# Layer-1 local attention: low weight pieces moved behind the exponentials and the scaling, pair 6's norm factor ahead of the last square, pair 7's sums and mean ahead of an output tile

## What is computed

```python
def swa_mixer(h, wq, wk, wv, q_norm_w, k_norm_w, sinks, wo):
    q = rms_norm((h @ wq).reshape(b, l, kv, grp, d), q_norm_w) * (d ** -0.5)
    k = rms_norm((h @ wk).reshape(b, l, kv, d), k_norm_w)
    v = (h @ wv).reshape(b, l, kv, d)
    ...
    s_meta = jnp.einsum('bnikgd,bjkd->bnkgij', qb, km)
    s_band = jnp.einsum('bnikgd,bnjkd->bnkgij', qb, kband)
    s_band = jnp.where(valid, s_band, -jnp.inf)
    p = sink_softmax(jnp.concatenate([s_meta, s_band], -1), sink)
    orr = (jnp.einsum('bnkgim,bmkd->bnikgd', p[..., :N_META], vm)
           + jnp.einsum('bnkgij,bnjkd->bnikgd', p[..., N_META:], vband))
    return jnp.concatenate([om, orr], 1) @ wo
```

## Time and profile before

| | |
|---|---|
| median of 3 runs | 1246.34 us (1246.31 to 1250.26) |
| profiled execution | 1246.21 us, of which its span 1244.4 us |
| PE busy | 1219.0 us (98%), 9378 matmuls |
| DVE busy | 897.7 us (72%) |
| ACT busy | 695.2 us (56%) |
| POOL busy | 179.7 us (14%) |
| chain that ended last | PE 89%, DVE 6%, ACT 3% of the span |

### The profile page before, as it was taken

One profiled execution on the slowest core, in us unless ns is written; L12 is line 12 of the kernel. 1 busy time (PEld: TensorE's weight loads), 2 busy tenths in 40 slices (PEclk: granted clock), 3 DMA queues, 4 the chain that ended last, 5 costly groups with the idle time before them and its releaser, 6 DMA issues.

```text
span 1244.4 us, 25767 instructions
## 1 busy us (share of the span) xinstructions
PE 1219.0 (98%) x9378; PEld 1136.2 (91%) x9378; DVE 897.7 (72%) x1670; ACT 695.2 (56%) x1272; POOL 179.7 (14%) x214
## 2 busy tenths in 40 slices
PE   7999999999999989999999999999999999999997
PEld 7999999999999889999989999888889879888887
DVE  7688688788546869888756667977555797877453
ACT  7667355555434656555544555777444586777432
POOL 0343150000112333000011004000011105000100
PEclk9999999999999999999999999999999999999999
DMA  8323357776544336566654444666666523665662
GB/s 293 103 86 110 96 152 236 205 200 198 190 154 120 103 121 207 183 185 196 209 167 146 132 147 145 199 185 186 189 185 183 186 83 120 201 186 170 202 186 69
DMA packets 60449, 205.80 MB, mean 165 GB/s; under 512 B 6096, under 2 KB 14544, under 8 KB 60240
## 3 DMA queue, kind: packets, MB, share of 16 engines
q1 hardware_dynamic: 56048, 200.33, 52.5%
q10 hardware_dynamic: 4320, 4.35, 1.1%
HBM read 200.46 MB, written 4.19 MB: 164 GB/s over the span
## 4 chain that ended last, share of the span: by engine, by line
PE 89%; DVE 6%; ACT 3%; issue 1%; POOL 0%; DMA 0%; ACTq 0%; DVEq 0%
PE bank L331 27%; PE bank L327 21%; PE bank L329 17%; PE bank L330 17%; DVE w_lo L279 1%; DVE cb L700 1%; PE bank L1642 1%; PE bank L1619 1%; PE bank L1632 1%; ACT w_hi L270 1%; ACT sm_s L1699 1%; DVE sm_d L1657 0%; ACT sm_d L1699 0%; PE bank L1294 0%; DMA raw<-w_mix_in 0%
## 5 line engine op out<-in xcount | busy, mean ns | idle before, releaser
L279 DVE TENSOR_TENSOR w_lo<-raw,w_hi 128x1024 fp32r<-128x1024 f32 (+1 forms) x357 | 461.1, 1293 | 167.1 <-ACT w_hi L270 166.5
L331 PE MATMUL bank<-x,w_lo 128*128 128x256 f32 (+2 forms) x1776 | 503.8, 284 | 0.0
L270 ACT ACTIVATE w_hi<-raw 128x1024 fp32r<-128x1024 f32 (+1 forms) x357 | 386.1, 1084 | 207.5 <-PE bank L331 198.5
L329 PE MATMUL bank<-x,w_hi 128*128 128x272 f32 (+2 forms) x1264 | 365.5, 289 | 8.0 <-DVE x L405 8.0
L330 PE MATMUL bank<-x,w_hi 128*128 128x272 f32 (+2 forms) x1264 | 360.4, 285 | 0.0
L331 PEld LDWEIGHTS bank<-x,w_lo 128*128 128x128 f32 x1776 | 334.5, 188 | 0.1
L329 PEld LDWEIGHTS bank<-x,w_hi 128*128 128x128 f32 x1264 | 239.0, 189 | 10.2 <-DVE w_lo L279 8.0
L330 PEld LDWEIGHTS bank<-x,w_hi 128*128 128x128 f32 x1264 | 238.8, 189 | 0.4
L327 PE MATMUL bank<-x,w_hi 128*128 128x512 f32 x512 | 181.4, 397 | 0.0
L327 PE MATMUL bank<-m,w_hi 128*128 128x512 f32 x448 | 157.4, 393 | 0.0
L331 PE MATMUL bank<-m,w_lo 128*128 128x256 f32 x512 | 144.8, 283 | 0.0
(11 more groups left out here) (338 smaller groups left out, 1784.6 us busy)
## 6 DMA issues: line engine op xcount, KB each, us to landing
raw<-w_up SPq DMA_DIRECT2D x88, 512.0 KB, 4.3
raw<-w_mlp_up SPq DMA_DIRECT2D x64, 512.0 KB, 4.2
raw<-w_mlp_down SPq DMA_DIRECT2D x64, 512.0 KB, 4.2
raw<-w_down SPq DMA_DIRECT2D x32, 704.0 KB, 4.1
raw<-w_mix_in SPq DMA_DIRECT2D x29, 512.0 KB, 3.9
raw<-w_moba_in SPq DMA_DIRECT2D x24, 512.0 KB, 4.3
raw<-w_swa_in SPq DMA_DIRECT2D x12, 512.0 KB, 3.6
raw<-w_mix_out SPq DMA_DIRECT2D x8, 512.0 KB, 3.5
```

Of the source, the lines that this page charges most:

```text
L270: nc.scalar.activation(w_hi[:, slot, 0:WIDTHS[g]], raw[:, slot, 0:WIDTHS[g]], ACT.Copy).then_inc(hi_ready, 1)
L279: nc.vector.tensor_tensor(w_lo[:, slot, 0:WIDTHS[g]], raw[:, slot, 0:WIDTHS[g]], w_hi[:, slot, 0:WIDTHS[g]].bitcast(F32), ALU.subtract).th ...
L329: nc.tensor.matmul(out, whi, xh, start=(chunk == 0), stop=False)
L331: mm = nc.tensor.matmul(out, wlo, xh, start=False, stop=end)
```

## The change

Three things move; no instruction is added or removed. First, in steps 1 to 5 ACT makes the `w_hi` piece after the exponentials, and in steps 0 to 5 DVE makes the `w_lo` piece after the scaling `norm`, ahead of the tile's eviction. Second, POOL takes pair 6's power ahead of the square of query tile 7. Third, PE does the head sums of pair 7 ahead of the partial output tile of step 6, and ACT takes their mean ahead of pair 6's exponentials.

```diff
@@ dve_swa @@
                     if p < 6:
+                        norm(p, 0, 2)
                         dve_rest(dve, lin.piece0 + (6 if p else 5) + p + AHEAD)
-                        norm(p, 0, 2)
                     else:
@@ act_swa @@
                 if p < HEADS // 2:
-                    if 0 < p < 6:
+                    if p == 6:
+                        squares_mean(p + 1)
+                    pair_exps(act, swa, p)
+                    if p < 6:
                         act_round(act, lin.piece0 + 6 + p + AHEAD)
-                    pair_exps(act, swa, p)
                     if p in (4, 7):
                         lag_copy(p // 7)
-                    if p == 0:
-                        act_round(act, lin.piece0 + 6 + AHEAD)
-                    if p + 1 < HEADS // 2:
+                    if p < 6:
                         squares_mean(p + 1)
-                    else:
+                    elif p == 7:
                         act.wait_ge(S("rel_stored"), 16 * 8)
@@ pool_swa @@
-                if 1 < t < 7:
+                if t > 1:
                     rsqrt(t - 1)
...
-            rsqrt(6)
             lag_queries(1)
@@ pe_swa @@
                 if p == 6:
+                    query_sums(p + 1)
                     pe.wait_ge(evac_done, SWA0 + 11)
                     pe_tile(pe, out, 0, ready=early, part=(0, 4))
...
-                if p + 1 < HEADS // 2:
+                if p < 6:
                     query_sums(p + 1)
```

## The result

| | before | changed |
|---|---|---|
| median (8 runs each) | 1246.72 us (1246.07 to 1250.26) | 1250.72 us (1248.40 to 1251.66) |
| profiled execution | 1246.21 us, span 1244.4 | 1248.40 us, span 1246.6 |
| ratio | | 1.0022, interval 1.0012 to 1.0032 |

The change makes the kernel about 0.2% slower. The two medians alone have a ratio of 1.0032, the upper end of the interval. I measure local attention from PE's first scores (402.37 in the profile before, 402.19 in this one) to DVE's first residual tile behind it (459.40 and 461.58): 57.03 us before, 59.39 now, +2.36.

The account below looks back on a forecast made before the run. PE was taken to bound the kernel, waiting only for DVE's lag rows. Weight moves +2.7 to +2.9 us and about -0.7 from the other edits gave +2.1: 1248.3 or 1248.5, forecast 1248.5 us, range 1246.4 to 1250.3.

Parts of the forecast that it names:

- DVE's round: DVE's time per step in local attention: from 5.11 to 6.25 us, against 6.29 for PE's own step.
- the lateness of step 0: Two pieces follow step 0's scaling instead of one: reduction 1 moves from 409.42 to 410.56 and DVE never catches up.
- The turn of step 4: PE's turn after `lag_max` in step 3: at 429.82 instead of 427.30, 2.5 us late, PE idle about 2.2 us.
- The wait of step 2: PE's turn at 414.05 held about 0.7 us by scaling 1, its first new wait.
- Steps 4 and 5: PE's next turns at 436.93 and 443.22, both 2.7 us late.
- The bank wait: New PE wait of 0.9 us before pair 7's head sums, until ACT copies the small transpose out of bank 7.
- The turn of step 7: PE's turn after `lag_max(1)`: at 449.6 against 447.46, 2.1 us late, carried to the end.
- the tail's two edits: Steps 6 and 7: power ahead -1.5 us on DVE, sums ahead +0.9 on PE, together about -0.7.
- The weight moves: Moving `w_hi` and `w_lo` in steps 0 to 5 alone costs 2.7 to 2.9 us.
- The first: Weight moves cost nothing in local attention; only the -0.7 us of the tail stays: 1245.6 us; chance 0.10.
- the second: Each of six moved pieces costs PE its full 1.14 us: +6.1 us, 1252.4 us; chance 0.05.
- The third: PE's clock falls in the 2.2 us gap, one slow tile adds 2.4 us: +4.5, 1250.8 us; chance 0.05.

Follow-up runs that it names:

- step 0 undone: Changed kernel with step 0's `w_lo` piece put back between the reduction and the scaling; ratio to the kernel before 1.0011, lowest run +1.5 us.
- DVE alone: Kernel before with only DVE's `w_lo` pieces moved behind the scaling, ACT's `w_hi` still ahead of the exponentials; ratio 1.0048, lowest run +6.1 us.
- ACT alone: Kernel before with only ACT's `w_hi` pieces moved behind the exponentials, DVE's `w_lo` still ahead of the scaling; ratio 1.0056, lowest run +6.7 us.

## Why the prediction was right, and where it was off

- **DVE's round.** Predicted to grow from 5.11 to 6.25 us; measured 6.25 and 6.27. Reductions 1, 2 and 3 were forecast at 410.56, 416.81 and 423.06 and came at 410.37, 416.62 and 422.89 (the stretch began 0.18 us earlier). That the lateness of step 0 is never caught up is shown by undoing step 0 alone.
- **The turn of step 4.** Forecast 429.82, measured 429.65, for the lag maximum; PE's idle time 2.18 us (about 2.2). The wait of step 2 came as 0.54 us plus a turn longer by 0.13, for 0.7.
- **Steps 4 and 5.** Forecast turns 436.93 and 443.22, measured 436.74 and 443.03. One thing in between was not foreseen: POOL's power of pair 5 took 2.26 us (434.55) rather than 1.04, as in one of the two other profiles of this kernel, and held reduction 5 by 0.16 us; it cost nothing, since ACT held the exponentials anyway.
- **The bank wait.** Forecast 0.9 us before the sums of pair 7, measured 0.79. The turn of step 7 was forecast at 449.6 and came at 449.66. Relative to the start of the stretch that is +2.4, not +2.1: the tail's two edits were mis-sized. I had -0.7 for them; the power alone gives -1.2 to -1.3, the sums and the mean +0.8, so -0.35 to -0.5 remains. With the earlier start put back, the turn came at 449.84 and not 449.6; of these 0.24 us, 0.08 lie at the end of the bank wait (444.98 for 444.9) and 0.12 in PE's work from the sums to the last values (444.80 to 448.34, for 3.42 us). The forecast did not see that `lag_max(1)` waited 0.58 us for POOL in the kernel before. In the changed kernel POOL's factor for these rows is there by 448.12 and binds nothing. The weight moves were forecast at +2.7 to +2.9 and give +2.8.
- **Rivals.** The first (weight moves free) is refuted by their run alone, the second (each piece in full, +6.1) by the changed kernel, though each half of the weight moves alone does cost 5 to 6 us. The third, the clock, was put as an alternative with a chance of 0.05 and a price of 2.4 us. The lower level in that price was read from the matmuls of the first tile alone, 0.22 to 0.23 us apart; the granted clock reads 1.00 there, so that row does not bear it out. The fall is in truth an addition in part of the runs: it is seen in one of three profiles of the changed kernel, at 1.04 us net. The term was mis-sized, since the low clock ended before the tile did and part of the slow time fell into the next wait, and it was wrongly tied to a gap longer than any before: the gap of 1.87 us in the kernel before does the same.
- **The sum.** The profiled execution came at 1248.40 us where 1248.3 was forecast. The median of 1250.72 us lies above the forecast of 1248.5, and above 1250.3, the top of the range. By the ratio of 1.0022, on the 1246.34 us that the forecast started from, the time would be 1249.1, inside it. I had also given 0.86 to a change that cannot be told from none, and the interval of the ratio leaves out 1. What the sum lacks is a term for a clock that falls in part of the runs; that was left to rival 3. The six runs above 1250 us have a mean granted clock of 0.995 to 0.996, the two at 1248.4 and 1248.5 have 0.998, as have the profiles in which the clock fell nowhere but at the very end. How many of those falls belong to the new gap and how many to the first layer, where both kernels have them (in 2 of 3 profiles of before and 1 of 3 of the changed kernel), is not settled, as only a profile tells where the clock fell.

## What to carry to other kernels

A piece of background work is free where its engine waits anyway; ask of every move whether the old place was such a wait and whether the new one is on the way to the next hand-over. Add up the engine's round before and after and compare it with the bound engine's step, as lateness below that limit vanishes and lateness at it stays to the end. When two operations share a bank, keep enough work between them to cover the copy that frees it; moving the sums up opened a wait of 0.79 us here.

## What the runs showed of the hardware

Gaps of PE of 1.8 to 2.3 us were followed by the lower clock level in some executions and not in others, with the same queues: in the profiles of this study 7 of 13 such gaps (before 1.88, 1.87, 1.87 us: the last one; changed 2.18, 2.18, 2.19: the second; weight moves 2.18 and 2.05: both; step 0 undone 1.81: yes; DVE alone 2.20 and 2.27: the second; ACT alone 1.95 and 2.28: the first). Behind the shorter waits of this stretch (1.44 us at most) no fall was seen. Each of the falls whose cost could be read lasted some 3 us and cost 1.0 to 1.2 us net, from turn to turn, after the short wait next behind it (0.30 or 0.40 us without a fall) had been filled.

A gap of this length is not needed for a fall. At 126 to 134 us in the first layer six of the thirteen profiles show one, with no wait of PE recorded ahead of it: the granted clock is 0.57 over the 8 us in three of them (that of before at 1250.09 us is one), and 0.66 over 126 to 131 us in the three others (that of before at 1247.64 us is one). The fall at 989 to 994 us came behind waits of 0.57 and 0.62 us. So what makes the clock fall in one execution and not in the next stays open. The Trainium skill (page "TensorE: Matmul & The Clock Gate", section "What's actually happening") has the clock released by activity and throttled again after idle time. The profiles agree with that behind 7 of these 13 gaps; the fall in the first layer, with PE recorded busy, they do not explain by idle time.
